# Down projection of a gated MLP: 7 of 22 weight tiles as 2x2 block products in seven products (Strassen form), block sums made on VectorE

## The reference

```python
D_MODEL, SEQ, D_FF = 2048, 256, 5632
def conv_gated_ffn(h, w_up, conv_w, conv_b, w_down):
    u = h @ w_up
    up = jnp.pad(u, ((0, 0), (CONV_W - 1, 0), (0, 0)))
    c = conv_b + sum(up[:, j:j + S] * conv_w[j] for j in range(CONV_W))
    gate, val = c[..., :D_FF], c[..., D_FF:]
    return (jax.nn.silu(gate) * val) @ w_down
x = x + conv_gated_ffn(h, w_up[l], conv_w[l], conv_b[l], w_down[l])
return rms_norm(x, norm_final)
```

## Time and profile before

| | us |
|---|---|
| median of 3 runs (1082.51 to 1083.49) | 1083.16 |
| the profiled execution | 1082.85 |
| its span, first to last instruction | 1081.1 |

### The profile page before, as it was taken

One profiled execution on the slowest core, in us unless ns is written; L12 is line 12 of the kernel. 1 busy time (PEld: TensorE's weight loads), 2 busy tenths in 40 slices (PEclk: granted clock), 3 DMA queues, 4 the chain that ended last, 5 costly groups with the idle time before them and its releaser, 6 DMA issues.

```text
span 1081.1 us, 17621 instructions
## 1 busy us (share of the span) xinstructions
PE 1070.0 (99%) x6005; PEld 916.5 (85%) x6005; DVE 722.3 (67%) x1058; ACT 587.6 (54%) x909; POOL 9.5 (1%) x30
## 2 busy tenths in 40 slices
PE   8999999999999999999999999999999999999997
PEld 8888888888888888888888888888888888888885
DVE  5677777686555777777787777778777445454543
ACT  6956475755545655556556655555556444343432
POOL 1000000000000000000000000000000000000000
PEclk9999999999999999999999999999999999999999
DMA  9575555554556566566655666566666655555552
GB/s 290 172 233 168 177 162 175 161 169 158 173 177 190 179 194 191 176 185 203 193 184 169 208 191 195 180 178 206 189 184 213 213 190 185 192 192 182 191 194 97
DMA packets 171329, 201.64 MB, mean 187 GB/s; under 512 B 8580, under 2 KB 138340, under 8 KB 171168
## 3 DMA queue, kind: packets, MB, share of 16 engines
q1 hardware_dynamic: 170576, 199.59, 59.0%
q0 software_dynamic: 400, 1.27, 0.4%
q10 hardware_dynamic: 320, 0.34, 0.1%
HBM read 199.06 MB, written 2.11 MB: 186 GB/s over the span
## 4 chain that ended last, share of the span: by engine, by line
PE 98%; DMA 1%; SPq 0%; DVE 0%; ACT 0%; issue 0%; DVEq 0%
PE tr_ps L1295 15%; PE pj L1295 15%; PE pj L1047 9%; PE pj L1297 8%; PE tr_ps L1297 8%; PE sc_ps L1035 5%; PE sc_ps L1037 5%; PE sc_ps L1036 5%; PE pj L1049 4%; PE tr_ps L1037 4%; PE tr_ps L1036 4%; PE tr_ps L1035 4%; PE pj L1062 3%; PE pj L1036 2%; PE pj L1035 2%; PE pj L1037 2%
## 5 line engine op out<-in xcount | busy, mean ns | idle before, releaser
L686 DVE TENSOR_TENSOR split<-raw,split 128x1024 fp32r<-128x1024 f32 x366 | 443.3, 1223 | 266.1 <-ACT split L409 260.5
L409 ACT ACTIVATE split<-raw 128x1024 fp32r<-128x1024 f32 x360 | 376.1, 1057 | 234.9 <-PE sc_ps L1037 78.9
L1295 PE MATMUL tr_ps<-act_split,split 128*128 128x512 f32 x704 | 245.3, 391 | 0.0
L1295 PE MATMUL pj<-act_split,split 128*128 128x512 f32 x704 | 245.0, 391 | 0.0
L1297 PE MATMUL pj<-act_split,split 128*128 128x256 f32 x704 | 197.1, 280 | 0.0
L1297 PE MATMUL tr_ps<-act_split,split 128*128 128x256 f32 x704 | 197.1, 280 | 0.0
L1295 PEld LDWEIGHTS pj<-act_split,split 128*128 128x128 f32 x704 | 131.7, 187 | 28.8
L1295 PEld LDWEIGHTS tr_ps<-act_split,split 128*128 128x128 f32 x704 | 131.7, 187 | 28.8
L1047 PE MATMUL pj<-act_split,split 128*128 128x512 f32 x416 | 147.6, 399 | 0.0
L1297 PEld LDWEIGHTS tr_ps<-act_split,split 128*128 128x128 f32 x704 | 133.1, 189 | 0.1
L1297 PEld LDWEIGHTS pj<-act_split,split 128*128 128x128 f32 x704 | 133.1, 189 | 0.0
(11 more groups left out here) (200 smaller groups left out, 1179.6 us busy)
## 6 DMA issues: line engine op xcount, KB each, us to landing
raw<-w_up SPq DMA_DIRECT2D x176, 512.0 KB, 4.5
raw<-w_down SPq DMA_DIRECT2D x88, 512.0 KB, 4.4
raw<-w_in SPq DMA_DIRECT2D x72, 512.0 KB, 3.7
raw<-w_o SPq DMA_DIRECT2D x32, 512.0 KB, 3.8
nat<-x SPq DMA_DIRECT2D x8, 256.0 KB, 5.9
key_bias<-nft_dram SPq DMA_DIRECT2D x4, 512.0 KB, 4.9
result<-nat SPq DMA_DIRECT2D x7, 256.0 KB, 3.1
gfin<-norm_final POOLq DMA_DIRECT2D x1, 1024.0 KB, 7.6
```

The lines of the kernel that those rows point to most:

```text
L409: act.activation(hi[:, slot, 0:TILE], raw[:, slot, 0:TILE], ACT.Copy).then_inc(hi_done, 1)
L686: dve.tensor_tensor(lo[:, slot, 0:n], raw[:, slot, 0:n], hi[:, slot, 0:n].bitcast(F32), ALU.subtract).then_inc(lo_done, 1)
L1295: pe.matmul(up_banks[v][b].rearrange("p (a n) -> p a n", a=2), wh[:, c, b * P:(b + 1) * P], act_split[:, :, k, :], start=k == 0, stop=Fals ...
```

## The change

The order of the stage is now a list of 116 steps, `DOWN`, in two groups `g` of 1024 output columns. In a group, 15 of the 22 row tiles are **plain**, in two halves of 512 columns, as before: 12 matmuls a step. The other seven (kt = 2, 4, ... 14) are **sums blocks** of four steps: the two loaded tiles of that kt (left and right 512 columns, parts 0 and 1) and two steps that are not loaded (parts 2 and 3), whose raw slots DVE fills with sums. With A the values (2x2 blocks of 128 features by 128 tokens) and W the weights (2x2 blocks of 128x512) the seven products go into the banks `p1` to `p7`:

- part 0: A11 by W11 into p1, A12 by W21 into p2 (6 matmuls)
- part 1: S4 by W22 into p3 (3 matmuls; of this tile only the second chunk is split, 128x512 in place of 128x1024)
- part 2: S1 by T1 and S3 by T3 (6 matmuls)
- part 3: S2 by T2 and A22 by T4 (6 matmuls)

The T are made by `add_weights`, four additions of 128x512 on DVE (L1085, L1086, L1089, L1091), ahead of the split of part 0, once both loads of the block have landed and the remainder of the step before is done. The S are made once, in group 0, by `add_values` (L1058, L1063, L1067, L1069: 512, 256, 128 and 128 columns) and split by `sums_hi` on ACT and `sums_lo` on DVE (L1075) into `s_hi` and `s_lo`; group 1 uses them again. After a group's last block, `combine` spreads ten operations of 128x512 over five steps. All steps go through the same ring of four, at number t. Between the blocks of group 0 lie 4, 3, 4, 3, 4 and 4 plain steps, between those of group 1 always 3. After the last block of group 0 come 4 plain steps, of group 1 come 8. The sums and their splits lie where the up projection's input was; `gfin` moves to the up step's buffers, and POOL's load of it waits for the last `glo_s` of the up projection in place of the last matmul. SP's 88 loads are unrolled.

```diff
--- before.py
+++ after.py
-T_END = T_DOWN + GROUPS * DOWN_TILES
+SUM_KT = (2, 4, 6, 8, 10, 12, 14)
+PLAIN_KT = tuple(kt for kt in range(DOWN_TILES) if kt not in SUM_KT)
+SUMS_AFTER = ((3, 7, 10, 14, 17, 21, 25), (3, 6, 9, 12, 15, 18, 21))
...
+def down_plan():
+    plan = []
+    for g in range(2):
+        for i, (half, kt) in enumerate((half, kt) for half in range(2) for kt in PLAIN_KT):
+            plan.append((g, "plain", half, kt))
+            if i in SUMS_AFTER[g]:
+                plan += [(g, "sums", part, SUM_KT[SUMS_AFTER[g].index(i)]) for part in range(4)]
+    return plan
+DOWN = down_plan()
...
+        p1, p2, p3, p4 = tr_ps[:, 0], sc_ps[:, 0], pj[:, 2], sc_ps[:, 1]
+        p5, p6, p7, p8 = tr_ps[:, 1], pj[:, 0], pj[:, 1], pj[:, 3]
...
-            with sp.Fori(0, GROUPS // 2) as g:
-                for k in range(2 * DOWN_TILES):
-                    n, kt = divmod(k, DOWN_TILES)
-                    load(g * (2 * DOWN_TILES) + (T_DOWN + k), k % RING, wide(raw, k % RING),
-                         wdn[kt][:, :, bass.ds(g * 1024 + n * 512, 512)])
+            for t, (g, kind, part, kt) in enumerate(DOWN):
+                if loaded(DOWN[t]):
+                    load(T_DOWN + t, t % RING, wide(raw, t % RING),
+                         wdn[kt][:, :, (2 * g + part) * 512:(2 * g + part + 1) * 512])
...
-            pool.wait_ge(mm_done, T_DOWN)
+            pool.wait_ge(glo_s, UP_STEPS)
...
+            def down_hi(t):
+                slot = t % RING
+                g, kind, part, kt = DOWN[t]
+                c0 = 512 if kind == "sums" and part == 1 else 0
+                if loaded(DOWN[t]):
+                    act.wait_ge(d_w[slot], slot_loads(t))
+                else:
+                    act.wait_ge(sum_s, 4 * sums_index(t - part) + 2 * part - 2)
+                act.wait_ge(mm_done, T_DOWN + t - (RING - 1))
+                act.activation(hi[:, slot, c0:TILE], raw[:, slot, c0:TILE], ACT.Copy).then_inc(hi_done, 1)
+            def sums_hi(q):
+                act.wait_ge(s_fp, 4 * q + 4)
+                act.activation(s_hi[:, q], sums[:], ACT.Copy).then_inc(shi_s, 1)
+            for t in range(DOWN_END):
-                if 0 < t and T_DOWN + t + LEAD < T_END:
-                    split_hi(T_DOWN + t + LEAD, (t + LEAD) % RING)
-                if t % DOWN_TILES == DOWN_TILES - 1 and t < 3 * DOWN_TILES:
-                    squares(t // DOWN_TILES)
+                if t == 1:
+                    sums_hi(0)
+                if 0 < t and t + LEAD < DOWN_END:
+                    down_hi(t + LEAD)
+                if 1 < t < GROUP_END[0] - 5 and DOWN[t + 5][:3] == (0, "sums", 0):
+                    sums_hi(sums_index(t + 5))
...
+            def down_lo(t):
+                slot = t % RING
+                g, kind, part, kt = DOWN[t]
+                c0 = 512 if kind == "sums" and part == 1 else 0
+                dve.wait_ge(hi_done, T_DOWN + t + 1)
+                dve.tensor_tensor(lo[:, slot, c0:TILE], raw[:, slot, c0:TILE], hi[:, slot, c0:TILE].bitcast(F32),
+                                  ALU.subtract).then_inc(lo_done, 1)
+            def add_values(q):
+                kt = SUM_KT[q]
+                blocks = slice(2 * kt, 2 * kt + 2)
+                if q > 0:
+                    dve.wait_ge(s_fp, 4 * q)
+                dve.tensor_tensor(whole[:], g_hi[:, blocks].rearrange("p b n -> p (b n)").bitcast(F32),
+                                  g_lo[:, blocks].rearrange("p b n -> p (b n)").bitcast(F32), ALU.add).then_inc(s_fp, 1)
+                dve.wait_ge(s_fp, 4 * q + 1)
+                if q > 0:
+                    dve.wait_ge(slo_s, q)
+                dve.tensor_tensor(sums[:, 0:2 * P].rearrange("p (a n) -> p a n", a=2),
+                                  whole[:, 0:2 * P].rearrange("p (a n) -> p a n", a=2),
+                                  whole[:].rearrange("p (b m n) -> p b m n", b=2, m=2)[:, :, 1], ALU.subtract).then_inc(s_fp, 1)
+                dve.wait_ge(s_fp, 4 * q + 2)
+                dve.tensor_tensor(sums[:, 2 * P:3 * P], sums[:, 0:P], whole[:, 3 * P:4 * P], ALU.add).then_inc(s_fp, 1)
+                dve.wait_ge(s_fp, 4 * q + 3)
+                dve.tensor_tensor(sums[:, 3 * P:4 * P], whole[:, 2 * P:3 * P], sums[:, 2 * P:3 * P],
+                                  ALU.subtract).then_inc(s_fp, 1)
+            def sums_lo(q):
+                dve.wait_ge(shi_s, q + 1)
+                dve.tensor_tensor(s_lo[:, q], sums[:], s_hi[:, q].bitcast(F32), ALU.subtract).then_inc(slo_s, 1)
+            def add_weights(t):
+                q = sums_index(t)
+                (w11, w21), (w12, w22) = [[raw[:, (t + r) % RING, c * 512:(c + 1) * 512] for c in range(2)] for r in range(2)]
+                (t1, t3), (t2, t4) = [[raw[:, (t + r) % RING, c * 512:(c + 1) * 512] for c in range(2)] for r in range(2, 4)]
+                for r in range(2):
+                    dve.wait_ge(d_w[(t + r) % RING], slot_loads(t + r))
+                dve.wait_ge(lo_done, T_DOWN + t - 1)
+                dve.tensor_tensor(t1, w11, w12, ALU.add).then_inc(sum_s, 1)
+                dve.tensor_tensor(t3, w12, w22, ALU.add).then_inc(sum_s, 1)
+                dve.wait_ge(sum_s, 4 * q + 1)
+                dve.wait_ge(lo_done, T_DOWN + t)
+                dve.tensor_tensor(t2, t1, w22, ALU.add).then_inc(sum_s, 1)
+                dve.wait_ge(sum_s, 4 * q + 3)
+                dve.tensor_tensor(t4, t2, w21, ALU.add).then_inc(sum_s, 1)
...
+            def combine(g, step):
+                c11, c21, c12, c22 = [nat[:, m, (2 * g + n) * 512:(2 * g + n + 1) * 512] for n in range(2) for m in range(2)]
+                if step == 0:
+                    dve.wait_ge(mm_done, T_DOWN + SUMS_END[g])
+                    dve.tensor_tensor(c11, p2, c11, ALU.add).then_inc(comb_s, 1)
...
+                if step == 1:
+                    dve.wait_ge(comb_s, 8 * g + 1)
+                    dve.tensor_tensor(c11, c11, sums[:], ALU.add).then_inc(z_s, 1)
+                    dve.wait_ge(comb_s, 8 * g + 2)
+                    dve.wait_ge(z_s, 4 * g + 5)
+                    dve.tensor_tensor(sums[:], whole[:], p7, ALU.subtract).then_inc(comb_s, 1)
+                    dve.tensor_tensor(c21, p4, c21, ALU.add).then_inc(comb_s, 1)
...
+            dve.wait_ge(glo_s, UP_STEPS)
+            dve.wait_ge(mm_done, T_DOWN)
+            for t in range(DOWN_END):
+                if t == 1:
+                    add_values(0)
+                if t > 1 and t + 5 < GROUP_END[0] and DOWN[t + 5][:3] == (0, "sums", 0):
+                    add_values(sums_index(t + 5))
+                if t > 1 and t + 4 < GROUP_END[0] and DOWN[t + 4][:3] == (0, "sums", 0):
+                    sums_lo(sums_index(t + 4))
+                if 0 < t and t + LEAD < DOWN_END:
+                    if DOWN[t + LEAD][1:3] == ("sums", 0):
+                        add_weights(t + LEAD)
+                    down_lo(t + LEAD)
+                if t == 1:
+                    sums_lo(0)
+                for g in range(2):
+                    if SUMS_END[g] <= t < SUMS_END[g] + 5:
+                        combine(g, t - SUMS_END[g])
...
+            def down_sums(t):
+                g, kind, part, kt = DOWN[t]
...
+                if part == 0:
+                    down_mm(p1, *g_part(A11), slot, 0, q == 0)
+                    ins = down_mm(p2, *g_part(A12), slot, 1, False)
+                elif part == 1:
+                    ins = down_mm(p3, *s_part(S4), slot, 1, q == 0)
+                elif part == 2:
+                    down_mm(p5, *s_part(S1), slot, 0, q == 0)
+                    ins = down_mm(p7, *s_part(S3), slot, 1, q == 0)
+                else:
+                    down_mm(p6, *s_part(S2), slot, 0, q == 0)
+                    ins = down_mm(p4, *g_part(A22), slot, 1, False)
...
-            for n in range(GROUPS):
-                for kt in range(DOWN_TILES - (LAST if n == 3 else 0)):
-                    if n == 0:
-                        pe.wait_ge(glo_s, kt + 1)
-                    if kt == 0:
-                        pe.wait_ge(z_s, 2 * n + 2)
-                    pe.wait_ge(lo_done, T_DOWN + n * DOWN_TILES + kt + 1)
-                    down(n, kt, range(MT)).then_inc(mm_done, 1)
+            for t in range(DOWN_END - LAST):
+                g, kind, part, kt = DOWN[t]
+                if g == 0:
+                    pe.wait_ge(glo_s, kt + 1)
+                if t == GROUP_END[0]:
+                    pe.wait_ge(comb_s, 4)
+                if DOWN[t][1:3] == ("sums", 0) and kt == SUM_KT[0]:
+                    if g == 0:
+                        pe.wait_ge(u_s, 4 * UP_STEPS)
+                    else:
+                        pe.wait_ge(comb_s, 8)
+                        pe.wait_ge(z_s, 8)
+                if g == 0 and kind == "sums" and part == 1:
+                    pe.wait_ge(slo_s, SUM_KT.index(kt) + 1)
+                pe.wait_ge(lo_done, T_DOWN + t + 1)
+                if kind == "plain":
+                    ins = down(t, range(MT))
```

(43 more changed lines are left out.)

96 lines of the change are left out of this document (69 added, 27 removed).

## The result

The changed kernel takes **1093.64 us** (median of 6 runs, 1091.23 to 1095.29), the kernel before 1083.15 in the same session (6 runs, 1082.51 to 1083.50): a ratio of 1.0094, 95% interval 1.0080 to 1.0108. It is slower by 10.5 us. The forecast was 1096.5, in a range of 1081 to 1112, with 0.83 on slower.

What follows compares the result with a forecast made beforehand. PE was taken as the bound, with everything waiting for it. Waits of 23.5 us less 9.8 us of removed matmuls gave +13.7 us on the profiled 1082.85, so 1096.5 us, in a range of 1081 to 1112.

Steps and rivals of the forecast that it cites:

- Removed, -9.8: Down projection on PE: 42 matmuls go, at 0.2324 us each, -9.8 us.
- The chain of a distance in group 1, 14.9: Two weight loads landing in turn, with copy, remainders and additions, take 14.9 us against PE's 13.25; PE waits 1.65.
- Group 1, 9.9 and 1.8 for the gain operations: PE's waits in group 1: six distances at 1.65 us, 9.9; gain operations in DVE's queue in the first two, 1.8.
- Group 0, 3.3, 2.6 and 0.5: PE's waits in group 0: two short distances 3.3 us, four long 2.6, 0.5 more in the first, DVE catching up.
- The load of gfin, 1.0: POOL's 1 MB load starts some 7 us later and meets the first block's weight loads; 0 to 2, taken as 1.0 us.
- Turn of the groups, 1.4: Between the groups, combining operations and residual additions on DVE make PE wait 1.4 us, 0.65 behind the last block.
- Start, 1.9: Start of the down projection: DVE's value sums and additions precede step 4's remainder, so PE loses 1.9 us, restart included.
- After the last block, 1.1: Behind group 1's last block the first plain step is ready at 6.03 + 0.15, PE there at 5.03: 1.1 us.
- A: Rival: down weight loads in a burst queue harder, 2.1 us each, +14.4 us, about 1111; chance 17%.
- B: Rival: the group 1 load chain hides behind PE, landings 3.4 + 3.4; faster, about 1077; chance 10%.
- C: Rival: quick loads in the group 1 chain but single operation durations; about no change, 1081 to 1085; chance 8%.
- D: Rival: PE's clock drops to the lower level during the waits in some 13 places, giving 1116; chance 3%.

Runs made afterwards that it cites:

- run 6: Against the changed kernel with weight sums in buffers of their own: later blocks and first value sums in group 0, group 1 distances respaced; 1073.30 us, 0.9906.

## Why the prediction was right

The mechanism, its place and its direction were right: the ring's two lost slots make a block's loads late, in group 1 with two landings in a row, and PE waits on the plain step behind the block. The sizes were less good. The forecast had 23.5 us of loss, the stage lost 19.8. Marked by DVE's first additions, the stage lost 1.7 at the start, 8.1 in group 0, -0.6 at the turn, 8.9 in group 1 and 1.3 after the last block, 19.4 in all. The two large misses, group 1 (11.7 forecast) and the turn (1.4), lay on the same side; group 0 came out 0.7 over its 7.4.

These are DVE's marks. Where PE itself stood still is a little different, as two of its restarts in the changed kernel tell:

```profile
947.58 0.47 PE L1220 MATMUL pj<-split,g_hi 128*128 128x512 f32 x1 [0.68 <-DVE split L1049]
...
992.50 0.50 PE L1220 MATMUL sc_ps<-split,g_hi 128*128 128x512 f32 x1 [0.37 <-DVE split L1049]
```

The first is behind the last block of group 0, the second behind the second block of group 1. Behind the first block of group 1 PE does not wait at all. What DVE caught up at the turn was a store ahead, and the first distance of group 1, 15.28 long, used it up. The prediction had said that there is no such store. Start to start, with the restarts, PE lost 1.8 at the start, 8.5 in group 0, 0.9 at the turn, 6.4 in group 1 and 1.3 after the last block, and 1.0 in delays too short for the list of waits. So group 1 was forecast 5.3 too high, and the turn 0.5.

- **Removed, -9.8.** As forecast: 5963 matmuls, and run 6 gives back 10.0 with almost no wait. Whoever stops here forecasts 1073.
- **The chain of a distance in group 1, 14.9.** The six first additions lie 15.28, 14.90, 14.67, 14.20, 14.95 and 14.42 apart, mean 14.74. The sum is closer than its terms. The first load, which I let land in 3.5 because its queue had been quiet, took 4.1. The four behind it I let land 1.8 us apart. From the first landing (1016.62) to the fifth (1022.85) are 6.23 us, 1.6 each. Time 0, the end of the first remainder, is 1011.27 + 1.22 = 1012.49, and SP's load starts 0.03 behind it, not 0.16. So the fifth lands 10.4 after time 0, where 10.86 was forecast: +0.6 for the first landing, -0.1 for the issue and -1.0 for the four behind it partly cancel, which is luck. DVE operations back to back also overlap a little: four additions span 1008.73 to 1011.27, 2.54, where I had 2.76.
- **Group 1, 9.9 and 1.8 for the gain operations.** With 13.25 taken off, the six distances lose 8.9. The first two, which carry the gain operations, lose 3.7, where 5.1 was forecast. The other four lose 1.3 each in place of 1.65, so some 1.1 of the two may be the gain's, for 1.8. I had added its operations to the chain in full, without asking how much of them falls in DVE's idle time.
- **Group 0, 3.3, 2.6 and 0.5.** The distances were forecast at 17.2, 14.9, 16.7, 14.9, 16.7, 16.7 and measured at 18.11, 14.60, 17.45, 14.71, 17.18, 16.67. Less PE's own 13.25 and 16.04 they lose 8.1, for 7.4 with gfin. The short ones are 0.2 to 0.3 under. There the additions (871.28 and 903.44) wait for nothing: behind the first landing DVE worked without a gap, as the forecast said, so one landing and DVE's work set these two, and not two landings. Of the long ones the first is 0.9 over, the third 0.75, the fifth 0.5. I had costed the long ones by DVE's work as well, but in these three the additions wait for the second tile's load (1.15, 0.24 and 1.04 us), which landed in 5.6, 4.7 and 5.5.
- **The load of gfin, 1.0.** This term was wrong, and its cause did not occur. The page of the changed kernel has

```profile
gfin<-norm_final POOLq DMA_DIRECT2D x1, 1024.0 KB, 5.0
```

 It was issued at 837.1 and had landed at 842.1. The weight load before it had landed at 831.8, and the next was issued at 842.35. It met none. Without it group 0 was forecast at 6.4 for the 8.1 measured; the 1.0 for gfin hid part of this miss.
- **Turn of the groups, 1.4.** From the last block of group 0 to the first of group 1 are 26.59 us, 2 less than my 28.6 and less than PE's own 27.2. DVE caught up there.
- **Start, 1.9.** The matmul of step 4 started at 842.47 and would have at 840.76 without a wait, 1.7. The value sums took 1.72 (1.75), their 128-column additions 292 ns (0.30). Run 6 moves these sums and the first block behind the start, and the wait falls to 0.43.
- **After the last block, 1.1.** The wait at 1062.66 is 1.05, with its restart 1.3.
- **Costed at nothing.** PE never waited for the splits of the value sums or for the combining operations, as said.
- **Rivals.** A needed 2.1 us a load; it was 1.6. B and C needed landings of 3.4 and 3.5 for both loads; in the distance read above they were 4.1 and 3.9, and in none of the six of group 1 was one of the two under 3.7. D: the clock stayed at 1.00 in the stage through 16 waits of up to 1.9 us, so the waits cost what they last and a restart, no more. The Trainium skill (TensorE: Matmul & The Clock Gate, section on HAM oscillation) describes a kernel in which the matmuls of each tile take less time than the wait for the next load, and the clock falls in every tile. This stage is not such a kernel: PE works 5 us or more between two waits, and the granted clock did not fall. The signs named for the forecast came: PE busy 94% in place of some 91%, waits on the plain step behind a block, L1085 waiting for a DMA in group 1. What the page shows as wait, 14.9 us, is under the 20 to 25 that I named. I had not counted that each wait hides some 0.27 of restart outside the column.

## What to carry to other kernels

A step that needs no load but takes a slot of the load ring makes the ring shorter for every load behind it; count how many landings then follow one another in a period, and compare their sum, with the copies and additions between them, with the bottleneck's work in that period, for total busy time (DVE 79%, DMA 53%) says nothing about it. Give sums made on chip a buffer of their own, so that loads run ahead at the ring's full depth, and put the first costly block where its producers have caught up. An idle or a waiting engine is worth nothing by itself: the additions waited more for their loads (13.1 us in all, for 7.7) in a version in which that wait cost next to nothing.
